# A ring of four raw expert matrices and five buffers of split halves, in place of five and four

## What is computed

```python
def hierarchical_moe(xn, w_rg, b_rg, w_re, b_re, w1, w3, w2):
    # top-1 group of 8 experts, then top-2 experts in it; 32 experts in all
    ...
    def block_ffn(args):
        tok, e = args
        xb = xt[tok]
        hb = jax.nn.silu(xb @ w1[e]) * (xb @ w3[e])
        return hb @ w2[e]
    ...
    y = jnp.einsum('nk,nkd->nd', gate.astype(xt.dtype), y_assign)
```

## Time and profile before

| | |
|---|---|
| median of 3 runs | 2600.47 us (2597.52 to 2601.3) |
| the profiled execution's own time | 2600.39 us |
| its span, first to last instruction | 2598.6 us |
| mean granted TensorE clock, share of 2.4 GHz | 0.978 |
| busy: PE, PEld, DVE, ACT, POOL | 2480.8, 1936.7, 1392.3, 1155.7, 112.1 us |
| loads of expert matrices | 99 of 2048 KB, issued from 1977.19 to 2524.0 us |

### The profile page before, as it was taken

How to read it: one execution, slowest core, us unless ns; L and a number is a source line. 1 busy time by engine, 2 the same in 40 slices (tenths; PEclk the granted TensorE clock), 3 DMA queues, 4 the chain that set the end, 5 groups by cost and what they waited for, 6 DMA issues and landing times.

```text
span 2598.6 us, 28452 instructions
## 1 busy us (share of the span) xinstructions
PE 2480.8 (95%) x11190; PEld 1936.7 (75%) x11190; DVE 1392.3 (54%) x1971; ACT 1155.7 (44%) x1578; POOL 112.1 (4%) x163
## 2 busy tenths in 40 slices
PE   7999999999999999999999999998999799999994
PEld 6867888888787788888887778887887566666663
DVE  5577444344434754434357463345345677777763
ACT  4388322123434742222233243333244677677762
POOL 0111000000140000000000000000000100000001
PEclk9989999999998999999999999999999999999997
DMA  4300333434331023232223122221314899999993
GB/s 147 130 1 14 101 114 101 159 98 136 133 122 41 2 81 122 73 122 85 89 70 130 65 86 90 108 97 65 123 42 178 354 426 431 428 430 427 429 402 126
DMA packets 147281, 414.33 MB, mean 159 GB/s; under 512 B 10667, under 2 KB 75334, under 8 KB 134342
## 3 DMA queue, kind: packets, MB, share of 16 engines
q1 hardware_dynamic: 141078, 391.17, 39.7%
q0 software_dynamic: 3296, 12.58, 1.3%
q10 hardware_dynamic: 2768, 8.69, 0.9%
HBM read 380.70 MB, written 31.72 MB: 159 GB/s over the span
## 4 chain that ended last, share of the span: by engine, by line
PE 77%; DVE 9%; DMA 7%; ACT 4%; issue 3%; POOL 0%; ACTq 0%; POOLq 0%; DVEq 0%
PE ps L321 20%; PE ps L322 20%; PE ps L323 20%; PE ps L2796 6%; DMA area<-in_w 5%; DVE area L2692 2%; PE ps L1003 1%; PE ps L1979 1%; PE ps L2734 1%; PE ps L2736 1%; PE ps L1686 1%; PE ps L969 1%; PE ps L1659 1%; PE ps L2128 1%; DVE actT_parts L2721 1%
## 5 line engine op out<-in xcount | busy, mean ns | idle before, releaser
L323 PE MATMUL ps<-area,area 128*128 128x512 f32 (+2 forms) x1712 | 660.9, 386 | 0.0
L346 DVE TENSOR_TENSOR area<-area,area 128x2048 fp32r<-128x2048 f32 (+4 forms) x161 | 341.2, 2120 | 553.9 <-ACT area L340 553.9
L340 ACT ACTIVATE area<-area 128x2048 fp32r<-128x2048 f32 (+4 forms) x161 | 284.3, 1766 | 557.6 <-PE ps L323 552.5
L322 PE MATMUL ps<-area,area 128*128 128x512 f32 (+3 forms) x1368 | 527.1, 385 | 0.0
L321 PE MATMUL ps<-actT_parts,area 128*128 128x512 f32 (+1 forms) x984 | 386.5, 393 | 7.7 <-DVE area L346 3.4
L322 PE MATMUL ps<-actT_parts,area 128*128 128x512 f32 (+1 forms) x984 | 383.6, 390 | 0.0
L323 PEld LDWEIGHTS ps<-area,area 128*128 128x128 f32 (+1 forms) x1712 | 321.3, 188 | 66.6
L2692 DVE TENSOR_TENSOR area<-area,area 128x2048 fp32r<-128x2048 f32 x132 | 300.0, 2284 | 18.1 <-ACT area L2687 17.5
L322 PEld LDWEIGHTS ps<-area,area 128*128 128x128 f32 x1368 | 259.3, 190 | 49.4
L321 PE MATMUL ps<-area,area 128*128 128x512 f32 (+2 forms) x728 | 277.8, 382 | 5.2 <-DVE area L744 5.2
L2687 ACT ACTIVATE area<-area 128x2048 fp32r<-128x2048 f32 x132 | 251.3, 1907 | 15.3 <-DMA area<-in_w 14.3
(11 more groups left out here) (344 smaller groups left out, 2679.7 us busy)
## 6 DMA issues: line engine op xcount, KB each, us to landing
area<-in_w SPq DMA_DIRECT2D x99, 2048.0 KB, 13.2
area<-in_w_in SPq DMA_DIRECT2D x16, 2048.0 KB, 7.6
area<-in_l_w_gate SPq DMA_DIRECT2D x22, 1024.0 KB, 5.2
area<-in_l_w_up SPq DMA_DIRECT2D x22, 1024.0 KB, 7.7
area<-in_l_w_in SPq DMA_DIRECT2D x9, 2048.0 KB, 8.0
expert_inputs<-maskz SPq DMA_DIRECT2D x24, 512.0 KB, 8.4
area<-in_l_w_down SPq DMA_DIRECT2D x8, 1536.0 KB, 6.8
area<-in_l_w_down SPq DMA_DIRECT2D x8, 1280.0 KB, 6.6
```

The source lines that it names most:

```text
L322: pe.matmul(dst(r), a.l, b.h, start=False, stop=False)
L323: m = pe.matmul(dst(r), a.h, b.l, start=False, stop=end)
L340: eng.activation(w.h, raw, ACT.Copy).then_inc(w_hi, 1)
L346: dve.tensor_tensor(w.l, raw, w.high_f, ALU.subtract).then_inc(w_lo, 1)
```

## The change

The ring of raw matrices gets four slots and the split halves five buffers. `PB` moves from word 20480 to 16384, `EX` stays at 36864. `early_work` stays in buffer 3, now at 28672. The split of piece 0 now writes words that still hold the router's halves, and is moved behind the wait for the router's product. SP loads matrices 3 to 5, not 3 to 6, before it waits for the sorted rows.

```diff
         if on(7):
-            NR, NPB = 5, 4
+            NR, NPB = 4, 5
             PB = NR * SLOT
             EX = PB + NPB * 2 * PIECE
...
             def router_act(act, ch):
                 act.activation(identR[:, :], ident[:, :], ACT.Copy).then_inc(m_id, 1)
+                act.wait_ge(mm, rw.m0 + 1)
                 split_high(act, 0)
-                act.wait_ge(mm, rw.m0 + 1)
                 norm.wait_col(act)
...
                 sp.wait_ge(mm, rw.m0 + 1)
-                for i in range(NS, 7):
+                for i in range(NS, 6):
                     load(i, order[i][0])
...
-                for i in range(7, 3 * NB):
+                for i in range(6, 3 * NB):
```

## The result

The changed kernel takes **2724.08 us**, the median of 4 runs (2720.78 to 2728.21), against 2600.89 us for the kernel before (the median of 4 runs, one more than in the table ahead of the prediction): 1.0475 times as long, 95% interval 1.0463 to 1.0488. It is slower by 123 us, the way that was forecast and inside the range, 26 us above the forecast of 2698.

A forecast was written before the change was run, and what follows sets the result against it. The DMA queue was taken to bound the expert loop; the changed ring would close a slower loop over one block. Forecast: 2600.4 + 81 (loop) + 17 (TensorE's clock) = 2698 us, range 2650 to 2737.

The forecast's parts named there:

- The queue bound the loop before: Expert loop before the change: paced by DMA bytes, 15.96 us a block at 427 GB/s, against 15.98 us in the trace.
- The fifth buffer gives 0 us: Buffers of split halves: a fifth loosens one wait by a piece; taken as 0 us, gain at most 14.3 us.
- The moved split costs 0 us: Piece 0's split behind the router's product: falls into 3.54 us of ScalarE idle time; 0 us, 1.9 us without that cover.
- The loads ahead of the loop cost nothing: Loads 4 and 5 before the loop: still issued before the rows are sorted; 0 us up to the end of down(0).
- The loop over one block, 18.69 us: Down(n-1)'s end, load (n+2,0)'s issue 0.04, landing 8.4, then 10.25 to down(n)'s end; 81 us over 30 blocks.
- The landing of 8.4 us: Time from issue to landing of load (n+2,0), taken from one such load issued at the end of down(0).
- TensorE's clock: Idle time ahead of downs lowers TensorE's clock; 1.70 us in 10 blocks, 17 us, bounds 0 and 51.
- The signs: Changed profile: downs 18.5 to 19 us apart, DMA share about 0.85, ScalarE load waits about 90 us, TensorE waits 2 to 4.
- The clock that stays up: Rival: same loop over one block, TensorE not slowed; 2682 us, chance 0.16.
- The shorter and the longer loop: Rivals on load (n+2,0): landing in 6.9 to 7.9 us, about 2650, chance 0.10; in 9.4 us, 2737, chance 0.15.
- The hidden loss: Rival: the DMA queue's depth hides one transfer less in flight, nothing changes; 2600 us, chance 0.05.
- the gain: Rival: fifth buffer lets ScalarE and VectorE split earlier, ScalarE's 14.3 us of waits go; 2586 us, chance 0.04.

The follow-up runs named there:

- ring5_copy_first: Kernel before (ring of five) with ScalarE's gate_low(n+1), turned_copy(n), silu(n+1) ahead of the split of load (n+2,0), VectorE's gate_sum likewise: 2597.7 us, ratio 0.999.
- ring4_buf4: Changed kernel with four buffers of halves in place of five, ring still of four slots: 2724.1 us, ratio 1.0489 to the kernel before.
- ring5_split_moved: Kernel before with only the split of piece 0 moved behind the router's product: 2602.7 us, ratio 1.0002.
- ring5_wait_down: Kernel before (five slots, four buffers) with one wait added: SP issues load (n,0) only when down(n-3) has ended: 2729.9 us, ratio 1.0496.
- ring4_copy_first: Changed kernel with ScalarE's gate_low(n+1), turned_copy(n), silu(n+1) ahead of the split of load (n+2,0), VectorE's gate_sum likewise: 2624.8 us, ratio 1.0096 to the kernel before.
- ring4_filled_wait: Changed kernel with unread matmuls on TensorE ahead of each down, four for even n, two for odd n: 2696.0 us, ratio 1.0379 to the kernel before.

## Why the prediction was right, and where it was short

- **The queue bound the loop before.** Borne out: the order that frees ScalarE brings nothing that can be measured in the ring of five (ring5_copy_first), and DMA stays at 1.01.
- **The fifth buffer gives 0 us.** Right within the noise (ring4_buf4). **The moved split costs 0 us.** Right, by the trace of ring5_split_moved. The prediction shows no row for its signal at about 1992.0 us; the trace before has the end of the product at 1991.99. **The loads ahead of the loop cost nothing.** Right: from the stage's first load to the end of down(0) it takes 75.8 us, before it was 75.6.
- **The loop over one block, 18.69 us.** Right in place and size. The wait alone gives the loss in a ring of five (ring5_wait_down); taking the copy out from behind the split takes back 99 of 123 us (ring4_copy_first); with the clock held the block is 18.81 us (ring4_filled_wait).
- **The landing of 8.4 us** was low by 0.2: 8.59 on average, 5.7 us in all. The median is 8.4, but 7 of the 30 took 9.0 to 9.9 us. Why just these is left open.
- **The term that was mis-sized is TensorE's clock: "two thirds of the 15 odd blocks, 10 x 1.70 = 17 us".** It measured 30 x (8.42 - 7.15) = 38 us, 21 more; with the landing's 5.7 that is the 27 us between forecast and profile. Two things were short, and both errors go the same way. The count: 18 slow downs, not 10. By n they are the even ones (what I called odd was the block that the idle time follows): 14 of the 15 even downs, which come after 3.5 to 5.2 us of idle, and 4 odd ones, after 1.9 to 3.1 us. And the price: I had one slow down of 8.85 us to go by; here they took 8.6 to 10.2.
- **The signs.** The share of the queue (0.83 for "0.85 or so") came as forecast, and TensorE's waits at the downs nearly so (1.6 to 5.2 us for "2 to 4"). ScalarE's waits for loads are 120 us where "about 90" was given. Downs do come unevenly, 18.5 to 22.8 us apart and not 18.5 to 19, but by the clock and the landing, on the same chain, and not by another loop.
- **The rivals.** The clock that stays up, 2682 us, is what ring4_filled_wait comes near to. The shorter and the longer loop differ by the landing; measured 8.6, near the forecast's. The hidden loss and the gain fell with the result itself, and ring5_wait_down and ring4_buf4 say why. The Trainium skill's fixed cost of about 2.0 us ("DMA: Bandwidth & Descriptors", anatomy of one DMA) is given there for DMAs that GpSimd issues, while SP issues these; it would make the landing an estimated 6.9 us. The shortest of the 30 took 8.2, so for these loads the measured time stands.

## What to carry to other kernels

The depth of a ring is not only a number of transfers in flight: with another size another consumer can be the one that frees a load's slot. Where that consumer is the last step of a block, and the same load stands ahead of that step in some engine's written order, the ring closes to a loop over one block, as it did here. Write down, for load i, who frees the slot of i - NR, and what stands behind load i's first use on its engine; a share of 1.01 of the queue doesn't show that danger. And price idle time ahead of a burst of matmuls twice: once as a wait and once for the clock that falls behind it.

## What the runs showed that I had not expected

- Matmuls without a use, some 0.86 us each, put into waits of 2.0 us (odd n) or 4.0 us (even n) on average, made a kernel 28 us faster: all 30 downs 7.1 us at a clock of 1.00, for 18 slow ones of 30 at 0.92.
- The clock fell after idle times of 1.9 and 2.2 us too, but not after each: down(5) took 8.83 us after 1.9 us of idle, while down(13) after 2.5 us and even down(2) after 3.6 us took 7.13. In ring5_wait_down, with idle times of much the same length (2.9 us on average, 3.0 here), 24 of the 30 downs were slow and not 18. So the length of one idle time didn't settle it, and what did is left open.
- A slow down can cost more than the one fall in the old trace showed: down(24) took 10.20 us after 4.4 us of idle.
- One split of 1.9 us, moved by two places in ScalarE's order, cost 44 us in the ring of five (2642.0 against 2597.7 for ring5_copy_first; 1.5 us a block over its 15.86), with the same instructions; the waits of the turn and the chain showed it.
